# Expert gathers of a two-layer mixture-of-experts stack: one indirect DMA of 8 KB rows per pick, or two of 4 KB rows into separate buffers

## What is computed

```python
def peer_ffn(x, norm_g, q_w, sub_keys, u, v):
    h = rmsnorm(x, norm_g).reshape(T, D)
    q = (h @ q_w).reshape(T, PEER_HEADS, 2, PEER_HALF)
    s = jnp.einsum('thcd,ckd->thck', q, sub_keys).astype(jnp.float32)
    ...
    idx = jnp.take_along_axis(cand_i, best_pos, axis=-1)
    gate = jax.nn.softmax(best_s, axis=-1).astype(x.dtype)
    def block(inp):
        hb, ib, gb = inp
        a = jnp.einsum('nd,nhkd->nhk', hb, u[ib])
        w = gb * jax.nn.gelu(a, approximate=False)
        return jnp.einsum('nhk,nhkd->nd', w, v[ib])
```

## Time and profile before

| what | value |
|---|---|
| median of 3 runs | 3040.3 us |
| lowest and highest | 3033.41 and 3043.57 us |
| the profiled execution, its own time | 3038.38 us |
| span in its profile, first to last instruction | 3036.6 us |
| busy PE, DVE, ACT, POOL | 2535.3, 1697.6, 1172.0, 945.1 us |
| DMA packets, data moved | 141949, 783.38 MB |

### The profile page before, as it was taken

The page is one execution under the profiler, slowest core; times in us unless marked ns, Lnnn a source line. Parts: engine busy times, 40 slices in busy tenths (PEclk is TensorE's granted clock), DMA queues, the critical chain, the costliest instruction groups (busy, mean ns, idle before and its releaser), DMA issues.

```text
span 3036.6 us, 35273 instructions
## 1 busy us (share of the span) xinstructions
PE 2535.3 (83%) x11858; PEld 1784.6 (59%) x11858; DVE 1697.6 (56%) x3591; ACT 1172.0 (39%) x2500; POOL 945.1 (31%) x736
## 2 busy tenths in 40 slices
PE   7999899999789999757788778777887777788777
PEld 7988799899669979646533333333655433333334
DVE  4552355555455524754377677665455467676663
ACT  4346533433553346434232323323353333223233
POOL 0014400000320058136333333332535333333333
PEclk9999899999889999878999998998888899989999
DMA  5543255455235555116799999997427899999993
GB/s 194 185 163 118 105 186 184 163 187 175 85 105 186 187 168 180 35 60 223 322 389 420 420 418 417 417 416 287 142 85 305 330 421 421 421 418 420 412 414 136
DMA packets 141949, 783.38 MB, mean 258 GB/s; under 512 B 15872, under 2 KB 16384, under 8 KB 76288
## 3 DMA queue, kind: packets, MB, share of 16 engines
q0 software_dynamic: 73728, 536.90, 42.8%
q1 hardware_dynamic: 65360, 237.44, 23.3%
q10 hardware_dynamic: 2736, 7.46, 0.8%
HBM read 780.69 MB, written 1.05 MB: 257 GB/s over the span
## 4 chain that ended last, share of the span: by engine, by line
PE 45%; DMA 25%; issue 10%; DVE 8%; ACT 6%; POOL 6%; POOLq 0%; SPq 0%; DVEq 0%; ACTq 0%
DMA arena<-experts,arena 25%; PE ps L436 12%; PE ps L437 11%; PE ps L438 11%; PE ps L878 5%; POOL ring_lo L310 4%; PE ps L881 4%; DVE arena L1874 3%; ACT row L1290 2%; ACT arena L1284 1%; POOL arena L1969 1%; DVE ring_lo L310 1%; DVE arena L1399 0%; POOL rs L1948 0%; DVE hT_lo L1460 0%
## 5 line engine op out<-in xcount | busy, mean ns | idle before, releaser
L878 PE MATMUL ps<-arena,row 128*128 128x512 f32 x1024 | 589.6, 660 | 316.3 <-ACT row L1290 316.3
L1874 DVE SCALAR_TENSOR_TENSOR arena<-arena,ps 128x1024 f32<-128x1024 f32 x512 | 612.4, 1218 | 277.0 <-DMA arena<-experts,arena 276.8
L1969 POOL DMA_INDIRECT arena<-experts,arena x512 | 486.3, 950 | 783.1 <-PE ps L881 537.9
L436 PE MATMUL ps<-hT_hi,ring_hi 128*128 128x256 f32 x2048 | 591.3, 289 | 5.9 <-DVE hT_lo L1460 5.2
L437 PE MATMUL ps<-hT_lo,ring_hi 128*128 128x256 f32 x2048 | 584.5, 285 | 0.0
L438 PE MATMUL ps<-hT_hi,ring_lo 128*128 128x256 f32 x2048 | 584.3, 285 | 0.0
L878 PEld LDWEIGHTS ps<-arena,row 128*128 128x128 f32 x1024 | 200.3, 206 | 625.0 <-ACT row L1290 411.5
L881 PE MATMUL ps<-arena,row 128*128 128x512 f32 x1024 | 567.5, 637 | 0.0
L310 POOL TENSOR_TENSOR ring_lo<-ring,ring_hi 128x1024 fp32r<-128x1024 f32 x180 | 433.9, 2418 | 293.9 <-ACT ring_hi L304 279.5
L304 ACT ACTIVATE ring_hi<-ring 128x1024 fp32r<-128x1024 f32 x448 | 462.8, 1057 | 154.5 <-PE ps L438 153.1
L436 PEld LDWEIGHTS ps<-hT_hi,ring_hi 128*128 128x128 f32 x2048 | 398.1, 194 | 14.7 <-issue 9.0
(11 more groups left out here) (260 smaller groups left out, 2950.8 us busy)
## 6 DMA issues: line engine op xcount, KB each, us to landing
ring<-stream SPq DMA_DIRECT2D x448, 512.0 KB, 3.4
arena<-experts,arena POOLq DMA_INDIRECT x512, 13.7
row<-rows_in ACTq DMA_DIRECT2D x11, 512.0 KB, 4.2
x<-x_in SPq DMA_DIRECT2D x1, 1024.0 KB, 4.8
out<-arena SPq DMA_DIRECT2D x2, 512.0 KB, 2.7
arena<-cols_in ACTq DMA_DIRECT2D x3, 256.0 KB, 2.7
cols<-cols_in SPq DMA_DIRECT2D x1, 425.5 KB, 5.4
arena<-cols_in ACTq DMA_DIRECT2D x1, 320.0 KB, 2.9
```

Of the source, the lines that this page charges most:

```text
L436: pe.matmul(dst, a[0], b[0], start=start, stop=False)
L878: lower = pe.matmul(ps[:, 2 * tb, :], diag, v[:, 0:HALF], start=first, stop=end)
L1874: last = dve.scalar_tensor_tensor(u, u, 1.0, h, ALU.mult, ALU.mult, accum_out=R["a"][:, n % 2, k:k + 1])
L1969: pool.indirect_dma_start(R["held"][:, g % HELD, :], None, experts, bass.IndirectOffsetOnAxis(ap=idx[:, n % 2, k:k + 1], axis=0))\
```

## The change

The table of experts is handed over as two, `expert_u` and `expert_v`, with rows of 4 KB. Each pick is gathered by two indirect DMAs of 128 rows of 4 KB (512 KB each) with the same indices: u into `held_u`, v into `held_v`, each with 11 slots and with semaphores of its own. POOL issues them in turn: u of a pick, then v of it. The u gather waits on `peer_a`, so on the dots of the whole group in which the slot's pick before was; the v gather waits on `expert_free`, as the 8 KB gather did. DVE waits for u alone. PE gets a wait of its own on v ahead of each pick's first matmul. The bytes in all are the same, and so is the space in SBUF.

```diff
-        expert_landed = [sem(f"expert_landed{i}") for i in range(HELD)]
+        u_landed = [sem(f"expert_u_landed{i}") for i in range(HELD)]
+        v_landed = [sem(f"expert_v_landed{i}") for i in range(HELD)]
...
-                       ("held", (HELD, EXPERT)))
+                       ("held_u", (HELD, D)), ("held_v", (HELD, D)))
...
-                        v = R["held"][:, (PICKS * l + TOPK * n + k) % HELD, D:]
+                        g = PICKS * l + TOPK * n + k
+                        v = R["held_v"][:, g % HELD, :]
+                        pe.wait_ge(v_landed[g % HELD], 16 * (g // HELD + 1))
...
-                        u = R["held"][:, g % HELD, 0:D]
-                        dve.wait_ge(expert_landed[g % HELD], 16 * (g // HELD + 1))
+                        u = R["held_u"][:, g % HELD, :]
+                        dve.wait_ge(u_landed[g % HELD], 16 * (g // HELD + 1))
...
+                        pick = bass.IndirectOffsetOnAxis(ap=idx[:, n % 2, k:k + 1], axis=0)
+                        if g >= HELD:
+                            pool.wait_ge(of("peer_a"), (g - HELD) // GROUP + 1)
+                        pool.indirect_dma_start(R["held_u"][:, g % HELD, :], None, expert_u, pick)\
+                            .then_inc(u_landed[g % HELD], 16)
                         if g >= HELD:
                             pool.wait_ge(of("expert_free"), g - HELD + 1)
-                        pool.indirect_dma_start(R["held"][:, g % HELD, :], None, experts,
-                                                bass.IndirectOffsetOnAxis(ap=idx[:, n % 2, k:k + 1], axis=0))\
-                            .then_inc(expert_landed[g % HELD], 16)
+                        pool.indirect_dma_start(R["held_v"][:, g % HELD, :], None, expert_v, pick)\
+                            .then_inc(v_landed[g % HELD], 16)
```

More of the change, by code:

```diff
@@ L124 @@
 ROWS = 11
-EXPERT = 2 * D
 UNITS = TB * PH
@@ L135, with build_program @@
            "kv": 9, "swa": 10, "peer1": 11, "ple1": 12}
-def build_program(nc, stream, experts, x_in, pos_in, cols_in, rows_in, out):
+def build_program(nc, stream, expert_u, expert_v, x_in, pos_in, cols_in, rows_in, out):
     n_blocks = AT["end"]
@@ L2104, in laid_out @@
     return {"stream": weight_stream(a),
-            "experts": np.concatenate([a["peer_u_2"], a["peer_v_2"]], 2).reshape(-1, EXPERT), "x_in": np.ascontiguousarray(a["x"][0]),
+            "expert_u": a["peer_u_2"].reshape(-1, D), "expert_v": a["peer_v_2"].reshape(-1, D), "x_in": np.ascontiguousarray(a["x"][0]),
             "pos_in": np.ascontiguousarray(pos.reshape(P, 2 * TB).astype(np.int32)),
```

## The result

The changed kernel takes **3063.2 us** (median of 5, 3061.9 to 3071.1) against 3040.3 us (5 runs, 3033.4 to 3043.8) in the job in which the result was taken. The ratio is 1.0086, with a 95% interval of 1.0065 to 1.0107. The forecast was 3078, with a range of 3043 to 3115. The profiled execution has a span of 3061.4 us, 24.8 more than the one before.

The account below looks back on a forecast made before the run. The prediction took the DMA engines, full with gathers in the two expert layers, to bound the kernel. 3038.4 us + 42.2 (4 KB packets) - 2.5 (layer ends), other terms 0, gave 3078 us, range 3043 to 3115.

Parts of the forecast that it names:

- The bound: Long stretches of both expert layers: DMA engines full with gathers, share 1.01 at 419 and 418 GB/s; POOL next.
- case A: The main forecast, DMA engines slowed by 4 KB packets: 3078 us, from 3060 to 3100, chance 0.61.
- Term 1: Saturated stretches: 4 KB packets move slower than 8 KB ones, +0.095 us a pick, +42.2 us over 444 picks.
- The upper end: Highest price of 4 KB packets, from the kernel's start with 4 KB loads alone at 403 GB/s: +0.105 us a pick.
- The 2 us for each DMA: The skill's fixed cost per DMA: 2.0 us more for each of 512 picks, some 4060 us in all; not adopted.
- Term 2: POOL's 512 more issues: 2.51 us a pick against 2.592 of DMA work, cost 0 with little cover.
- The index chain: POOL's wait on each unit's indices: 8.4 us left for pick 11's u gather to land, cost 0.
- Term 3: Slots and added waits of the gathers and PE: slots come free earlier against POOL's need, added waits cost 0.
- Term 4: Unit 0: 16 more gathers (20.1 us) between POOL's `make_lo`s fill existing waits, cost 0; without that cover 20 us a layer.
- Term 5: Ends of the two expert layers: DVE needs only the last u, -1.25 us twice, -2.5 us.
- rival B: Saturated stretches: POOL becomes the bound, at 1.35 us an issue +90 us, 3126 us, chance 0.2.

Follow-up runs that it names:

- after_long_op: The changed kernel with one 128x1 power operation on POOL ahead of each pick: 3277.0 us (4 runs), ratio 1.0767.
- quarters_2k: The changed kernel with each half gathered in two, so four gathers of 2 KB rows a pick from four tables: 4295.2 us (one run).
- after_extra_op: The changed kernel with one 128x1 memset on POOL ahead of each pick: 3069.7 us, ratio 1.0081.
- after_exp_low: The changed kernel with ACT's exponential for unit 1 ahead of unit 0's last two queries and POOL's `make_lo`s one gather group later: 3219.0 us, ratio 1.0568.

## Why the prediction was right, and where not

- **The bound** was named rightly: DMA share 1.02 in the long stretches, u dots 2.56 us apart, POOL busy about twice as long with its waits for PE nearly gone, PE without a wait for v. That the DMA engines and not POOL set the pace is shown by the end of the layer, where u goes on landing every 2.56 us with POOL done. The time is near the lower end of case A (3060 to 3100).
- **Term 1** was mis-sized: +0.095 us a pick expected, +0.074 measured, so 33 us instead of 42.2. The row that I took it from the earlier trace rows read well: 1.038 is the ratio of the rates per busy DMA engine there, and the long windows give 25.87 against 24.83 GB/s, 1.042. The step that failed came after it. I turned that ratio into time as if the share stayed where it was, but it rose from 1.010 to 1.023 of the gathers' queue, and 1.042 / 1.013 is the 1.029 by which a pick grew. The upper end, from the earlier trace rows, rests on a row that moves between 398 and 415 GB/s with nothing changed in it. By the Trainium skill (DMA: Bandwidth & Descriptors, "Specifications") 512 B is enough for line rate, so there would have been no cost; the traces differ from that by 0.074 us a pick. The 2 us for each DMA of the Trainium skill (same page, "Anatomy of one DMA — SWDGE (gpsimd) path", where the prediction names "Bandwidth") are not seen either: 512 more DMAs cost 25 us in all.
- **Term 2** holds: 2.48 us a pick of POOL work (2.51 in the prediction, which took the mean of an issue for the usual one) against 2.58 costs nothing, and after_long_op shows that the cover ends there. The index chain left 8.4 us from an issue's end to its landing, 9.3 from its start; the landing became 8.7 at the median and 10.4 at the most, which fits a queue that filled about as far as that chain allows.
- **Term 3**: slots are no limit (33.8 us of waits for PE), and u's own wait is worth some 2 us, within the noise.
- **Term 4**: POOL's waits ahead of `make_lo` in unit 0 took up the extra issues: 19.3 us of them became 0.2, against 20.1 us of issues. Unit 0 moved by +2.3 and -4.0 us, -1.7 in sum, for a cost of 0.
- **Term 5** can't be told apart: 33 - 2.5 is 30.5, and 27.7 us are in the stretches where both terms lie.
- **Missed** is the second level. My rival B had a like picture (share under 0.97), but its 3126 us is 100 us short of it, and the mechanism is another: POOL's issues stayed at 0.94 us, and the engines waited for semaphores. Against that level the range (up to 3115) would not have held; that the result was taken in one of the three jobs without it was luck.

## What to carry to other kernels

Where the DMA engines are full, splitting a transfer can cost rate, here 3% of the rate for 4 KB instead of 8 KB rows; the finer release that it bought was worth too little to measure. To tell whether the engines are full, look at whether transfers go on at the same pace once the issuing engine has stopped, and not at the share alone. Look at what the issuing engine has left after the split: two issues of 1.24 us under 2.58 us of transfer cost nothing where no semaphore was late, but the engine can then hardly make up a pause. And look for time where the full engine idles: one exponential moved past two blocks of queries brought 0.4% in the kernel before (and nothing sure in the changed one).

## What was not expected of the hardware

- A packet is not a row. Rows of 8 KB went as packets of 8 KB, rows of 2 KB in pairs as packets of 4 KB (131072 packets for 262144 rows in quarters_2k).
- The DMA share is no measure of the rate. It counts the packets' own time, and a packet of 4 KB took 164 ns on the mean in the long window of the changed kernel, 182 in that of after_long_op and 227 in that of quarters_2k, at 407, 346 and 209 GB/s: the share fell by less than the rate.
- An instruction of 0.12 us between two gather issues is free: the 0.30 us between them passes anyway (after_extra_op: 2.48 us from memset to memset).
- The issue takes 0.94 to 0.95 us at the median for 128 rows of 2, 4 or 8 KB alike.
- A semaphore can reach its waiter 5 us late, on three engines at once (after_exp_low), and in the same kernel in another job never: 3063 or 3225 us.
